# Retention taken head by head between the weight tiles of the second mixer's input projection

## The reference, cut to what matters

```python
z = h @ w_in_odd                      # 1024 -> 6144: q, k (4 x 256 each), v, g (4 x 512 each)
q = rope(q) * 256 ** -0.5;  k = rope(k)
# per head and chunk of L tokens (prompt: two chunks of 128, sample: one of 4 for each sequence)
scores = einsum('bihd,bjhd->bhij', q, k) * dmat
o = einsum('bhij,bjhe->bihe', scores, v) + einsum('bihd,bhde->bihe', q, s_prev) * q_decay
s_new = gamma ** L * s_prev + einsum('bjhd,bjhe->bhde', k * k_decay, v)
r = (o - mean(o)) * rsqrt(var(o) + EPS)          # over the 512 values of a head
out = (silu(g) * r) @ w_out_odd                  # 2048 -> 1024
```

## Time and profile before

| what | value |
|---|---|
| median of 3 runs | 1323.36 us (1316.52 to 1324.07) |
| profiled execution | 1325.95 us, of which the span from first to last instruction is 1324.2 us |
| TensorE busy | 1193.6 us (90%) |
| VectorE busy | 766.3 us (58%) |
| ScalarE busy | 584.3 us (44%) |
| GpSimd busy | 296.3 us (22%) |
| mean granted TensorE clock | 0.952 |
| DMA | 233.64 MB, mean 176 GB/s |

### The profile page before, as it was taken

The page is one execution under the profiler, slowest core; times in us unless marked ns, Lnnn a source line. Parts: engine busy times, 40 slices in busy tenths (PEclk is TensorE's granted clock), DMA queues, the critical chain, the costliest instruction groups (busy, mean ns, idle before and its releaser), DMA issues. The chain is left out here.

```text
span 1324.2 us, 22941 instructions
## 1 busy us (share of the span) xinstructions
PE 1193.6 (90%) x8557; PEld 1094.7 (83%) x8557; DVE 766.3 (58%) x1020; ACT 584.3 (44%) x940; POOL 296.3 (22%) x521
## 2 busy tenths in 40 slices
PE   6999998897999999699999667899999779999995
PEld 4999897677999999699997323699986679999994
DVE  3585735317888833766555655447445167888433
ACT  5456543335666544423345211255434156566442
POOL 4001201114555520200000111003001135465302
PEclk9999999988999999799999888899999789999998
DMA  9647566632554356344444987747747334444431
GB/s 215 232 133 257 176 200 196 236 121 68 178 169 160 112 165 205 102 159 159 138 149 150 339 299 260 254 152 262 245 144 247 139 103 152 160 163 144 149 126 36
DMA packets 177267, 233.64 MB, mean 176 GB/s; under 512 B 5374, under 2 KB 153226, under 8 KB 177200
## 3 DMA queue, kind: packets, MB, share of 16 engines
q1 hardware_dynamic: 159088, 169.09, 39.3%
q0 software_dynamic: 18112, 63.60, 13.8%
HBM read 207.50 MB, written 25.16 MB: 176 GB/s over the span
## 5 line engine op out<-in xcount | busy, mean ns | idle before, releaser
L392 PE MATMUL ps<-hh,wh 128*128 128x288 f32 x1600 | 487.2, 304 | 34.7 <-DVE hl L450 28.2
L327 DVE TENSOR_TENSOR wl<-raw,wh 128x2048 fp32r<-128x2048 f32 (+2 forms) x154 | 331.7, 2154 | 314.4 <-ACT wh L324 314.4
L392 PE MATMUL ps<-hl,wh 128*128 128x288 f32 x1600 | 480.0, 300 | 0.0
L392 PE MATMUL ps<-hh,wl 128*128 128x288 f32 x1600 | 478.2, 299 | 0.0
L324 ACT ACTIVATE wh<-raw 128x2048 fp32r<-128x2048 f32 (+3 forms) x154 | 277.7, 1803 | 296.6 <-PE ps L392 283.5
L392 PEld LDWEIGHTS ps<-hh,wh 128*128 128x128 f32 x1600 | 307.2, 192 | 41.5 <-issue 33.7
L392 PEld LDWEIGHTS ps<-hh,wl 128*128 128x128 f32 x1600 | 309.0, 193 | 0.0
L392 PEld LDWEIGHTS ps<-hl,wh 128*128 128x128 f32 x1600 | 308.3, 193 | 0.3
L392 PE MATMUL ps<-aH,wh 128*128 128x288 f32 x352 | 104.2, 296 | 0.0
L392 PE MATMUL ps<-aL,wh 128*128 128x288 f32 x352 | 103.8, 295 | 0.0
L392 PE MATMUL ps<-aH,wl 128*128 128x288 f32 x352 | 103.6, 294 | 0.0
(11 more groups left out here) (286 smaller groups left out, 1649.4 us busy)
## 6 DMA issues: line engine op xcount, KB each, us to landing
raw<-w_ffn_up SPq DMA_DIRECT2D x44, 1024.0 KB, 5.1
raw<-w_in_odd SPq DMA_DIRECT2D x24, 1024.0 KB, 5.2
ring<-cache_mem_k POOLq DMA_DIRECT2D x16, 1024.0 KB, 5.6
ring<-cache_mem_v POOLq DMA_DIRECT2D x16, 1024.0 KB, 5.7
raw<-state_retention SPq DMA_DIRECT2D x16, 1024.0 KB, 7.3
out<-raw POOLq DMA_DIRECT2D x16, 1024.0 KB, 6.2
raw<-w_ffn_down SPq DMA_DIRECT2D x16, 768.0 KB, 4.5
raw<-w_in_even SPq DMA_DIRECT2D x10, 1024.0 KB, 6.7
```

What stands on the lines that cost most here:

```text
L327: e.tensor_tensor(wl[:, c % 2, 0:kn, :], src, wh[:, c % 2, 0:kn, :].bitcast(F32), ALU.subtract).then_inc(lo_ready, 1)
L392: mm = pe.matmul(out, lhsT, rhs, start=(kc == 0 and n_k == 0 and n == 0), stop=(kc == g.nk - 1 and n_k == kn - 1 and n == 2))
```

## The change

The input projection is taken head by head: `odd_cols` reorders the columns so that each head's q, k and v tiles (8 tiles, one *window* W) come together, four such windows, then the 16 gate tiles (windows 4 and 5). The retention of head h = W-1 is cut into pieces that TensorE issues in the middle of a tile (`amid`) or behind it (`behind`). The UNITS loop is gone.

The states move to a ring `st` of four buffers of one state each (512 KB), a *step* U = 8 h + b for one head of one sequence, used behind tile U + 10. SyncE issues the state loads between the weight loads: ahead of weight chunk n it loads the states U = 2n-13 and 2n-12, each after the store of U-4. GpSimd issues only the stores. A step takes both halves of one state: 16 records of 128 columns with weights of 128 x 32 (four quarters of the value width beside each other), then two products for the update. As the sample rows of one head now stand in four quarters, `select` puts them side by side with four more products per head. `rows_out`, `turned_samples` and a third set of moments per head are new for the same reason.

Gates are evacuated, passed through Silu and multiplied as they come (`gated`, `gated_high`, `gated_low`); the output projection starts with heads 0 and 1 (`g_lo`) and no longer waits for the last gates. The loop over steps 1 to 3 of `in_odd` is written out. The core of the diff:

```diff
+    def odd_cols(i, half):
+        if i >= 2 * RH:
+            return 2 * RH * RDK + RH * RDV + 2 * CW * (i - 2 * RH) + CW * half
+        if i % 2:
+            return 2 * RH * RDK + RDV * (i // 2) + CW * half
+        return RH * RDK * half + RDK * (i // 2)
...
-            G["in", l] = gemm("in_odd", a["w_in_odd"][l // 2])
+            G["in", l] = gemm("in_odd", a["w_in_odd"][l // 2], (8,), odd_cols)
...
-                    if g is G["out", 1] and (i, idx) in ((0, 2), (1, 0)):
-                        if i == 0:
-                            load_states(e)
-                        for slot in (2 * i, 2 * i + 1):
-                            e.wait_ge(s(f"SR_out{slot}"), 16 * (DEC_B // 2))
+                    if g is G["in", 1]:
+                        load_states(e, i * g.per + idx)
...
+        def load_states(e, n):
+            if n == 4:
+                e.wait_ge(s("a_free"), 1)
+            for U in range(RH * DEC_B):
+                if n == (4 if U < 4 else (U + 7) // 2 + 3):
+                    if U >= 4:
+                        e.wait_ge(s(f"SR_out{U % 4}"), 16 * (U // 4))
+                    e.dma_start(st[:, U % 4], state_dram(a["state_retention"], U)).then_inc(s(f"SR_in{U % 4}"), 16)
...
-            for n, (hp, c) in enumerate(UNITS):
-                for half in range(2):
-                    pool.wait_ge(s("SR_new"), 8 * n + 4 * half + 4)
-                    pool.dma_start(states_dram(ret_sample, n, half), states(n, half)).then_inc(s(f"SR_out{n % 2 * 2 + half}"), 16)
-                    if c == 1 and half == 0:
-                        pool.wait_ge(s("S2_ready"), 2 * hp + 2)
-                        pool.dma_start(ret_prompt[0, 0, hp].rearrange("(t p) e -> p t e", p=P), S2[:]).then_inc(s("S2_stored"), 16)
-            pool.wait_ge(s("S2_stored"), 16 * RH)
+            for U in range(RH * DEC_B):
+                h, b = divmod(U, DEC_B)
+                pool.wait_ge(s("SR_new"), 2 * U + 2)
+                pool.dma_start(state_dram(ret_sample, U), st[:, U % 4]).then_inc(s(f"SR_out{U % 4}"), 16)
+                if b == 5:
+                    pool.wait_ge(s("S2_ready"), 2 * h + 2)
+                    pool.dma_start(ret_prompt[0, 0, h].rearrange("(t p) e -> p t e", p=P), S1[:]).then_inc(s("S2_stored"), 16)
...
+            for n in range(TILES):
+                W, u = divmod(n, 8)
+                h = W - 1
+                prompt = 1 <= W <= RH
+                own = W < RH
+                U = n - 10
+                if prompt and u == 0:
+                    natural_values(h, 0)
+                if prompt and u == 1:
+                    sample_values(h)
+                if prompt and u == 2:
+                    first_state(h, 1)
+                if 0 <= U < RH * DEC_B:
+                    own_keys(U)
...
+                if n % 2:
+                    i, idx = divmod(n // 2, 2)
+                    split(act, *target(g, i, idx, i == g.steps - 1), True)
...
+            def update(U):
+                h, b = divmod(U, DEC_B)
+                for dt in range(2):
+                    dve.wait_ge(s("SU_ps"), 2 * U + dt + 1)
+                    x = st[:, U % 4, dt, :]
+                    dve.scalar_tensor_tensor(out=x, in0=x, scalar=gL(h, DEC_T), in1=ps[:, OS + dt, :],
+                                             op0=ALU.mult, op1=ALU.add).then_inc(s("SR_new"), 1)
...
+                if prompt and u in (3, 4):
+                    moments("P", h, u - 3)
+                if prompt and u in (6, 7):
+                    last_state(h, u - 6)
+                tiles_ready(dve, g, i, r // 2, r % 2)
+                if not own:
+                    e = n - 32
+                    if e >= 8:
+                        dve.wait_ge(s("gated"), e - 7)
+                    dve.tensor_tensor(gate(e), ps[:, tile_bank(n), 0:T], rstd[:], ALU.mult).then_inc(s("oz"), 1)
+                elif u < 4:
+                    turn(n, head(W, "qk"[u // 2]))
+                else:
+                    keep(n, W, u - 4)
+                if n == 0:
+                    for p in range(2):
+                        after(dve.memset(QM[p][:], 0.0))
+                if prompt and u in (3, 4):
+                    scaled_rows("P", h, u - 3)
+                if own and u == 5:
+                    scores(W)
+                if own and u == 6:
+                    sample_scores(W)
+                if 0 <= U < RH * DEC_B:
+                    update(U)
...
+                if n % 2:
+                    split(dve, *target(g, i, r // 2, i == g.steps - 1), False)
...
+            def sample_state(U):
+                h, b = divmod(U, DEC_B)
+                pe.wait_ge(s(f"SR_in{U % 4}"), 16 * (U // 4) + 16)
+                if b == 0:
+                    pe.wait_ge(s("QM_ready"), h + 1)
+                for dt in range(2):
+                    for j in range(4):
+                        mm = pe.matmul(ps[j * NS:(j + 1) * NS, OR, 0:P], QM[h % 2][:, dt, b * NS:(b + 1) * NS],
+                                       st[:, U % 4, dt, j * P:(j + 1) * P], start=False, stop=b == DEC_B - 1 and dt == 1,
+                                       skip_group_check=True, tile_position=(0, j * NS))
+                if b == DEC_B - 1:
+                    mm.then_inc(s("rows_ps"), 1)
+                pe.wait_ge(s("K4m_ready"), U + 1)
+                for dt in range(2):
+                    if U:
+                        pe.wait_ge(s("SR_new"), 2 * U - 1 + dt)
+                    pe.matmul(ps[:, OS + dt, :], K4m[:, U % 2, dt * P:(dt + 1) * P], V4[h % 2][:],
+                              start=True, stop=True).then_inc(s("SU_ps"), 1)
+            def select(h):
+                pe.wait_ge(s("rows_out"), h + 1)
+                if h < RH - 1:
+                    pe.wait_ge(s("V4_ready"), h + 2)
+                else:
+                    pe.wait_ge(s("rS_out"), h)
+                for j in range(4):
+                    mm = pe.matmul(ps[0:NS, OC, j * P:(j + 1) * P], ident[:, j * NS:(j + 1) * NS], rowsC[:], start=True, stop=True)
+                mm.then_inc(s("sel_ps"), 1)
...
+            def amid(n):
+                W, u = divmod(n, 8)
+                h = W - 1
+                if W >= 2 and u == 2:
+                    select(W - 2)
+                if 1 <= W <= RH:
+                    if u == 0:
+                        natural_values(h, 0)
+                    if u == 1:
+                        sample_values(h)
+                    if u == 2:
+                        chunk_state(h, 0, 1)
+                    if u in (3, 4):
+                        outputs(h, u - 3)
+                    if u in (5, 6):
+                        turned_rows(h, u - 5)
+                    if u in (6, 7):
+                        chunk_state(h, 1, u - 6)
+                if W < RH and u == 7:
+                    natural_keys(W)
+            def behind(n):
+                W, u = divmod(n, 8)
+                h = W - 1
+                if 1 <= W <= RH:
+                    if u == 0:
+                        natural_values(h, 1)
+                    if u == 1:
+                        chunk_state(h, 0, 0)
+                    if u == 2:
+                        within_samples(h)
+                if W >= 2 and u == 4:
+                    turned_samples(W - 2)
+                if W < RH and u == 5:
+                    scores(W)
+                if W < RH and u == 6:
+                    sample_scores(W)
+                if 0 <= n - 10 < RH * DEC_B:
+                    sample_state(n - 10)
+                if W < RH and u == 7:
+                    sample_keys(W)
+            for n in range(TILES):
+                c = g.first + n // 2
+                bank, j = tile_bank(n), n % 2
+                if j == 0:
+                    pe.wait_ge(lo_ready, c + 1 + CREDIT)
+                if n in (4, 5):
+                    pe.wait_ge(s("oz"), n - 3)
+                elif n in (46, 47):
+                    pe.wait_ge(s("S2_ready"), n - 39)
+                elif n >= 6:
+                    pe.wait_ge(s("oz"), n - 1)
+                for k in range(DT):
+                    if n == 0:
+                        pe.wait_ge(h_lo, DT * q + k + 1)
+                    w_h, w_l = wh[:, c % 2, k, j * P:(j + 1) * P], wl[:, c % 2, k, j * P:(j + 1) * P]
+                    for x, (lhsT, rhs) in enumerate(((w_h, hh[:, k, :]), (w_h, hl[:, k, :]), (w_l, hh[:, k, :]))):
+                        mm = pe.matmul(ps[:, bank, 0:T], lhsT, rhs, start=k == 0 and x == 0, stop=k == DT - 1 and x == 2)
+                    if k == 3:
+                        amid(n)
+                mm.then_inc(w_used, 1)
+                if n == 1:
+                    ssq(pe, 2 * q)
+                behind(n)
...
-                             need=lambda k: pe.wait_ge(s("rg_lo"), 9 + k // 8))
+                             need=lambda k: pe.wait_ge(s("g_lo"), k // 2 + 1),
+                             enter=lambda t: pe.wait_ge(s("oz"), TILES - 3 + t))
```

(72 more changed lines are left out.)

617 lines of the change are left out of this document (282 added, 335 removed).

## The result

The changed kernel takes 1278.46 us (median of 4 runs, 1276.65 to 1279.64) against 1323.71 us (4 runs): ratio 0.967 with a 95% interval of 0.964 to 0.970. That is 45 us faster where 27 were forecast, and 2.5 us outside the low end of the range. The profiled execution took 1276.65 us (span 1274.9 us), 49.3 us less than that of before.

A forecast was written before the change was run, and what follows sets the result against it. TensorE was taken to bound the input projection, a chain across engines the retention. Stage 275.7 us for 300.8 (-25.1), output projection -2.9 and +1.0: -27.0 us from the 1323.36 us median, so 1296 us; range 1281 to 1326.

The forecast's parts named there:

- the 48.6 us that could be saved: Old retention stage of 122.2 us: 37.0 us of TensorE waits and some 11.6 us of low clock and tail.
- the waits added: Merged input projection and retention stage: TensorE waits on VectorE or ScalarE for moved pieces, taken as 6 us.
- the 73.6 us "in full": Retention products moved among the input projection's tiles: TensorE has no gaps to hide them, so 178.6 + 73.6 = 252.2 us.
- The two bounds: Limits on added waits: 2.3 us from the projection's weight-split waits, 17.9 us from the old retention stage's two VectorE waits.
- the hand walk: Queues walked through window W = 2: VectorE ends the heaviest tile's items about 8 us after it, two tiles before needed.
- The straight line gives 0.60, entering costs 0.20 more: Sample rows on TensorE: 32 sets at 0.80 us replace 8 at 2.05 us, adding 9.2 us.
- SyncE and GpSimd at nothing: State loads between weight loads on SyncE and 36 GpSimd stores in place of 20: no cost, under cover of weight slots.
- the first rival: Weight loads on SyncE wait behind state stores, making tiles late: +45 us, 1341 us; chance 0.10.
- Output projection, -1.9 us net: Start of the output projection: full clock saves 2.9 us; the split of the last gates' second chunk costs 1 us.
- Rival 2: Sample rows: small matmuls cost their issue, 0.060 us per record, not their columns; +17.6 us against forecast, 1314 us; chance 0.17.
- Rival 3: Merged stage: VectorE's in-order queue sets the pace, TensorE waits 17.9 us in place of 6; 1308 us; chance 0.13.
- A cost per interruption, 100 pieces at 0.2 us: Tile stream of the merged stage: named as the easiest way to be wrong, 20 us for interrupting the tiles.

## Why the prediction was off

The mechanism was right and the cost side too high: of the 48.6 us that could be saved it gave 23.5 back to added work and waits, and the run shows 3.4 (48.6 - 45.2). The stage was forecast at 275.7 us and took 255.4, 20.3 less. Two terms of that side failed: the waits added (6 us taken, none came) and the 73.6 us "in full"; the sample rows were sized nearly right. Point by point:

- **What can be saved: right.** The table of waits is empty behind the start, and the run without traffic shows the load waits and the clock that fell with them.
- **"Waits added: I take 6 us": failed.** From its first matmul TensorE stood 4.2 us in the whole stage, where the old projection alone stood 5.0: -0.9 us, so 6.9 us of the miss. The two bounds were read from waits in other orders of work; the hand walk, which said that VectorE's items end two tiles before they are needed, was the better source and led to zero. The run with 38 us more on VectorE had 2.7 us.
- **"The straight line gives 0.60, entering costs 0.20 more": right for a set that stands alone**, 0.77 us for 0.80: 0.57 in its own row and 0.20 in the rows beside it. Ten of the 32 sets share their entry with the narrow group ahead of them and cost 0.57, so the sets take 22.6 us in place of 25.6: 3.0 us of the miss.
- **`select`: too dear.** The last of the four stands alone in its tile and lengthens it from 3.20 to 4.38 us; four at 1.18 are 4.7 us for 5.6, 0.9 us of the miss. `within_samples` has 0.4 us more in its own rows, for 1.2, but its entry can't be told from that of the set behind it.
- **"The 73.6 us add in full": failed in size.** What is left of the 20.3 us, 9.5 us, lies in the moved products, with the slow start and the small terms. The 73.6 us are the old units less their waits as the rows have them, but a wait costs more than its row: 0.22 us more in the run with fewer rows, and in the earlier trace rows a product that the next one's wait stands behind holds TensorE for 0.50 us, where one in a step without waits takes 0.23. The old units have three such waits each, 24 in all, so 5.3 to 6.5 us of their "work" went with the waits (an estimate from these rows; no run takes the waits away and leaves the order). For the other 3 to 4 us no run names the cause. The low clock at the start alone moves the first eight tiles (stage less late) between 37.0 and 39.8 us from run to run.
- **SyncE and GpSimd at nothing: right, under the cover named.** SyncE stood 175.6 us at stores and GpSimd's place as issuer made no difference. The lead of five tiles was enough, with a tile of a step at about 6 us; with two tiles less the first rival comes true, and costs 96 us, not 45. I put the difference down to the ring through ScalarE's queue and to the clock that fell to 0.88.
- **Bandwidth: right**, 253 GB/s over the late stage where I worked out 250; in a stretch of 347 TensorE did not wait.
- **Output projection, -1.9 us net: right**, 2.5 us shorter, at full clock, with no wait for the last gates.
- **Rival 2: refuted.** A set costs 0.77 us and not 1.35, and further records start 0.027 us apart. The 0.060 us of the earlier trace rows are not a price of a record as such. The Trainium skill ("TensorE: Matmul & The Clock Gate", section "Wait — 56ns, not 53.3ns?") also gives a floor of about 25 ns from start to start however small the matmul; these 27 ns agree with that, and its 62 ns, given for hardware decode switched off, are not what binds here.
- **Rival 3: refuted** by the doubled updates.
- **"A cost per interruption, 100 pieces at 0.2 us"**: not for pieces in the form of the tiles, which may cut a tile anywhere; yes for each change to the narrow form, at 0.34 us. The Trainium skill ("TensorEngine Tiling (Array Packing)", section "Key Properties") says that a change of the tiling mode drains the engine. The trace agrees in that the rows on both sides of a narrow set grow, by 0.09 and 0.11 us.

## What to carry to other kernels

When a chain of short dependent products is spread among dense work on the same engine, it gains its idle time and something more for each wait that goes (here some 0.22 us, an estimate), and its waits need not be charged again if a walk through the queues shows slack: test that walk by doubling the suspected engine's work. A cost read from a group's start to the next start leaves out what stands in the rows beside the group: price it by the same step with and without it, and not by the fall of the whole time, to which new waits and the clock add their own. Take sets of one narrow form together (here two at a time, 4.7 us more). Where a load is queued behind a store in front of other loads, find the distance at which it turns over, by moving it both ways: here it was free at five tiles and cost 96 us at three.

## What was not expected of the hardware

The change to the form of 128 x 32 weights and back costs 0.34 us, and more than half of that, 0.20 us, stands not in the row of the narrow set but in the rows on both sides of it. An idle stretch of 0.93 us lengthened its step by 1.15 us. The weights took 8.0 us to land in place of 5.2 when states were moved beside them, at 253 GB/s in the mean, and TensorE did not wait for them.
